# mLSTM entry: the gate columns and the broadcast products of the rows spread among the products of the token panel pair

## The reference, cut to what matters

```python
b = jnp.cumsum(lfc, axis=-1)
dmat = jnp.where(tri, b[..., :, None] - b[..., None, :] + ic[..., None, :], -jnp.inf)
m_t = jnp.maximum(jnp.max(dmat, axis=-1), m_inter)
s = jnp.einsum('bhtk,bhsk->bhts', qc, kc) * jnp.exp(dmat - m_t[..., None])
num = jnp.einsum('bhts,bhsv->bhtv', s, vc) + ...
den = jnp.sum(s, axis=-1) + ...
h = num / jnp.maximum(jnp.abs(den), jnp.exp(-m_t))[..., None]
```

## Time and profile before

| | us |
|---|---|
| runs | 2332.77, 2332.36, 2329.47 |
| median | 2332.36 |
| the profiled execution, its own time | 2332.38 |
| span of the profiled execution | 2330.7 |
| TensorE busy | 2268.5 (97%) |
| VectorE busy | 1605.5 (69%) |
| ScalarE busy | 1102.0 (47%) |

### The profile page before, as it was taken

How to read it: one execution, slowest core, us unless ns; L and a number is a source line. 1 busy time by engine, 2 the same in 40 slices (tenths; PEclk the granted TensorE clock), 3 DMA queues, 4 the chain that set the end, 5 groups by cost and what they waited for, 6 DMA issues and landing times.

```text
span 2330.7 us, 37481 instructions
## 1 busy us (share of the span) xinstructions
PE 2268.5 (97%) x13900; PEld 1973.0 (85%) x13900; DVE 1605.5 (69%) x2706; ACT 1102.0 (47%) x1748; POOL 112.1 (5%) x155
## 2 busy tenths in 40 slices
PE   9999999999999989999999999999999999999998
PEld 8998779998998779997777778888888888888888
DVE  6677857667667957777455554444546999988896
ACT  5443444445343354435555543334434666565664
POOL 0000000000000001112121201001000000000000
PEclk9999999999999999999999998999999999999999
DMA  8655126655564226664343521221221222222222
GB/s 328 228 199 181 64 100 245 232 205 200 208 230 166 82 100 217 228 222 82 73 71 74 72 99 64 73 73 64 73 82 64 91 90 81 81 81 90 81 99 91
DMA packets 83068, 301.88 MB, mean 130 GB/s; under 512 B 10404, under 2 KB 10788, under 8 KB 82468
## 3 DMA queue, kind: packets, MB, share of 16 engines
q1 hardware_dynamic: 78336, 284.72, 35.0%
q0 software_dynamic: 2048, 4.20, 3.2%
q10 hardware_dynamic: 2600, 11.81, 1.4%
HBM read 299.64 MB, written 1.05 MB: 129 GB/s over the span
## 4 chain that ended last, share of the span: by engine, by line
PE 78%; DVE 15%; ACT 4%; issue 3%; DVEq 0%; DMA 0%; ACTq 0%; another core or an unknown queue 0%
PE ps L749 49%; PE ps L797 12%; PE ps L861 4%; DVE wsplit L2158 3%; DVE work L2875 2%; PE ps L1365 2%; DVE work L2887 2%; PE ps L1226 1%; PE ps L1089 1%; PE ps L1103 1%; PE ps L764 1%; PE ps L1079 1%; DVE work L2907 1%; DVE work L2919 1%; ACT wsplit L1493 1%
## 5 line engine op out<-in xcount | busy, mean ns | idle before, releaser
L749 PE MATMUL ps<-hsplit,wsplit 128*128 128x256 f32 (+1 forms) x8376 | 1380.3, 322 | 26.8 <-DVE wsplit L2158 11.5
L749 PEld LDWEIGHTS ps<-hsplit,wsplit 128*128 128x128 f32 x8376 | 1205.6, 191 | 159.3 <-DVE wsplit L2158 18.4
L2158 DVE TENSOR_TENSOR wsplit<-ring,wsplit 128x1024 fp32r<-128x1024 f32 x465 | 576.3, 1241 | 344.4 <-ACT wsplit L1493 342.4
L1493 ACT ACTIVATE wsplit<-ring 128x1024 fp32r<-128x1024 f32 x463 | 488.6, 1058 | 514.5 <-PE ps L749 394.6
L797 PE MATMUL ps<-wsplit,fsplit 128*128 128x512 f32 x1056 | 256.5, 392 | 1.9 <-DVE fsplit L2292 1.7
L797 PEld LDWEIGHTS ps<-wsplit,fsplit 128*128 128x128 f32 x1056 | 192.6, 188 | 40.1 <-issue 3.3
L2254 DVE SCALAR_TENSOR_TENSOR work<-ring,work 128x1024 f32<-128x1024 f32 x96 | 120.3, 1253 | 1.1 <-DMA ring<-panels 1.1
L1573 ACT ACTIVATE work<-ps 128x256 f32<-128x256 f32 x88 | 33.8, 384 | 161.0 <-PE ps L749 161.0
L2378 DVE SCALAR_TENSOR_TENSOR work<-work,vec 128x256 f32<-128x256 f32 x240 | 100.9, 481 | 1.7
L749 PEld LDWEIGHTS ps<-wsplit,hsplit 128*128 128x128 f32 x768 | 96.0, 198 | 5.3 <-issue 3.8
L861 PE MATMUL ps<-work,ring 128*128 128x256 f32 x416 | 99.2, 387 | 0.0
(11 more groups left out here) (369 smaller groups left out, 2307.6 us busy)
## 6 DMA issues: line engine op xcount, KB each, us to landing
ring<-panels SPq DMA_DIRECT2D x539, 512.0 KB, 4.1
work<-latent_weights ACTq DMA_DIRECT2D x2, 2304.0 KB, 11.9
work<-rpb POOLq DMA_DIRECT2D x64, 64.0 KB, 6.6
work<-conditions ACTq DMA_DIRECT2D x6, 512.0 KB, 7.0
cst<-constants ACTq DMA_DIRECT2D x1, 1408.0 KB
work<-x SPq DMA_DIRECT2D x2, 512.0 KB, 4.8
work<-post_rows ACTq DMA_DIRECT2D x2, 512.0 KB, 4.0
cT<-ctx ACTq DMA_DIRECT2D x1, 1024.0 KB, 7.3
```

The lines of the kernel that those rows point to most:

```text
L749: ins = mm(out_, w(a), x(b), start=start and n == 0, stop=stop and n == 2, **kw)
L1493: af(wsplit[:, split_slot(name, n), 0, :], ring[:, slot, :], ACT.Copy).then_inc(high_ready, 1)
L2158: tt(parts[:, 1, :], ring[:, slot, :], parts[:, 0, :].bitcast(fp32), ALU.subtract)\
```

## The change

`token_pair` takes a function that it calls after each of its 32 steps. In `b_scores` the two broadcast products of each head no longer stand ahead of the token pair, but after its steps 1 and 4. In head 0 the 16 gate columns go from ahead of `b_scores` to after the pair's steps 0 to 15, one each, and write bank 2 in place of bank 7. The wait for `g_act_stage` moves from ahead of the pair to ahead of panel n0 + 1, which writes bank 2. The number of products and their shapes stay.

```diff
-            def token_pair(n, bank):
+            def token_pair(n, bank, between=None):
...
                         last = mm3(ps[:, bank + t // 2, (t % 2) * T:(t % 2 + 1) * T].rearrange("p (s c) -> p s c", s=2),
                                    lambda a: hsplit2[:, a, k, t * 128:(t + 1) * 128], lambda a: pair[:, :, a, k, :],
                                    k == 0, k == KD - 1)
+                        if between is not None:
+                            between(t * KD + k)
...
             pe.wait_ge(g_rows_stage, 2)
-            for which, src in enumerate((g_G, b_M)):
-                for t in range(4):
-                    for d in range(2):
-                        o = 32 * which + (2 * t + d) * 4
-                        last = mm(ps[:, 7, o:o + 4], src[0:4, d, t * 128:(t + 1) * 128], cst[0:4, K_ID:K_ID + 4],
-                                  start=True, stop=True)
-            last.then_inc(g_products_done, 1)
+
+            def gate_columns(j):
+
+                which, t, d = j // 8, j // 2 % 4, j % 2
+                ins = mm(ps[:, 2, 4 * j:4 * j + 4], (g_G, b_M)[which][0:4, d, t * 128:(t + 1) * 128],
+                         cst[0:4, K_ID:K_ID + 4], start=True, stop=True)
+                if j == 15:
+                    ins.then_inc(g_products_done, 1)
...
-                for d in range(2):
-                    last = mm(ps[:, 4 + d, :], cst[0:4, K_ID + h:K_ID + h + 1].to_broadcast([4, 128]), b_R[0:4, d, :],
-                              start=True, stop=True)
-                last.then_inc(b_rb_done, 1)
                 if h > 0:
                     pe.wait_ge(b_y_ready, h)
-                else:
-                    pe.wait_ge(g_act_stage, 2)
-                token_pair(7 + 10 * h, 6)
+
+                def between(j):
+
+                    if j in (1, 4):
+                        d = j // 4
+                        ins = mm(ps[:, 4 + d, :], cst[0:4, K_ID + h:K_ID + h + 1].to_broadcast([4, 128]), b_R[0:4, d, :],
+                                 start=True, stop=True)
+                        if d == 1:
+                            ins.then_inc(b_rb_done, 1)
+                    if h == 0 and j < 16:
+                        gate_columns(j)
+
+                token_pair(7 + 10 * h, 6, between)
...
                 full_panel("B", n0, ps[:, 1, :])
+                if h == 0:
+                    pe.wait_ge(g_act_stage, 2)
                 full_panel("B", n0 + 1, ps[:, 2, :])
...
-            flat = lambda n: ps[:, 7, 32 * n:32 * n + 32].rearrange("p (a h) -> p a h", a=8)
+            flat = lambda n: ps[:, 2, 32 * n:32 * n + 32].rearrange("p (a h) -> p a h", a=8)
```

## The result

The changed kernel takes 2347.05 us (median of 6 runs, from 2338.75 to 2350.08); the kernel before, measured beside it, 2330.91 (6 runs, 2327.44 to 2332.77). The ratio is 1.0063, 95% interval 1.0043 to 1.0082: 0.6% slower, about 15 us. The profiled execution took 2346.3 us, with a span of 2344.6.

The account below looks back on a forecast made before the run. The prediction took TensorE, busy in 97% of the span, as the bound. Head 0 +9.1, heads 1 to 3 +2.5 steady and +3.5 for falls made +15.1 on 2332.4: 2347.5 us, range 2334 to 2353.

Parts of the forecast that it names:

- (a): Head 0, gate block gone: the pair waits for VectorE's low half and starts 2.5 us after the previous pair's end.
- (b): Small products between token products: lone column 0.47 us at 2.4 GHz, 0.82 at 1.2; lone broadcast product 1.24 us.
- (c): Head 0's clock falls soon after the first broadcast product, returning 4.4 us after the last column: 34.5 us, +9.1.
- (d): Heads 1 to 3: pair waits for VectorE, +0.85 a head, +2.5 us; two clock falls instead of one, +3.5 us.
- (e): ScalarE and VectorE work behind head 0's pair stays hidden, ending at 1435.3 against the pair's 1435.8; no cost.
- A: Rival for the spread products: the seam is free, the clock still falls; head 0 +2.4 us, total 2335; chance 0.08.
- B: Rival for the spread products: the seam costs, the clock holds; +0.5 us, total 2332.9; chance 0.07.
- C: Faster rival: no seam cost, and token products between hold the clock up; total 2326.3 us; chance 0.05.

Follow-up runs that it names:

- the run with fours: The changed kernel, still with 4-row products, but four gate columns at a time after steps 3, 7, 11 and 15; 2336.55 us, ratio 1.0024.
- The full-row run: The changed kernel with gate columns and broadcast products contracting over all 128 rows instead of 4, constant operand zero in the rest; 2324.92 us, ratio 0.9985.
- the run with the broadcast products alone: The kernel before with only the broadcast products spread, after steps 1 and 4 of each pair; gate columns in a block ahead of the rotation; 2338.3 us, ratio 1.0029.

## Why the prediction was right

2347.5 us was forecast and 2347.05 measured. By its steps:

- *(a)* Start of head 0's pair 2.5 us after the previous one: 1399.58 - 1396.86 = 2.72. Right; TensorE waits there for VectorE's low half, as said.
- *(b)* A lone column 0.47 us at 2.4 GHz and 0.82 at 1.2: measured 0.50 and 0.81. A lone broadcast product 1.24: the steady 0.90 a head of the run with fours, against 0.85 forecast, bears it out. (Two sums of this step are off by 0.01: 1.23 and 0.83 come out of their terms.) The full-row run shows that it is a seam between row counts, and nothing of fp32 beside fp32r: there the column costs 0.22, its price in the block. The run with fours shows that it is paid once for each visit. The Trainium skill ("TensorE: Matmul & The Clock Gate", Part 3, what overlaps and what doesn't) has a weight load overlap a running matmul only where the row groups differ. The traces agree with it in part at most. Between 128 and 4 rows, which share rows 0 to 3, the load did not run ahead (1402.68, as its product), but with the same 128 rows on both sides it did (load 1408.07, product 1408.19). That 4 rows count as another row group than the 128 around them was the prediction's reading, and the lone columns' price contradicts it.
- *(c)* Head 0, 34.5 us: measured 34.02 and 33.98. The time at full clock was forecast as 3.5 us and was 3.8 and 2.8 in the two profiles; the low tail after the last column was forecast as 4.4 and was 3.9 and 2.2. The step's account of the clock was too simple: it put broadcast products and columns on one footing. The runs show two roles: over 4 rows, the broadcast products go ahead of the fall, and with columns behind them the clock stays down. And it had the clock return only with token products without a break, where in the run with fours it rose in the last group of columns.
- *(d)* Steady part +0.85 a head: right (+0.90). The falls were undersized: two in three heads at 2.5 us, +3.5 us over before. In both profiles all three heads fell, in the first for 10.2, 6.8 and 3.4 us, which by 16.77 for a head without a fall cost 4.5, 3.0 and 1.5 us; in the second 1.5 each. Heads 1 to 3 together lost 10.3 us in the first profiles (59.36 against 49.09) and 4.2 in the second (54.77 against 50.57), where 6.0 was forecast. This is the mis-sized term; with two profiles of each kernel its mean over executions stays open.
- *(e)* Hidden work stayed hidden, by 0.80 us where 0.5 was forecast. The full-row run shows that this cover has an end: there the pair is 14.5 us shorter, and 1.3 us of the chain show.

The total comes as close as 0.5 us by luck. The mechanism held in the main, but the changed kernel's own runs spread from 2338.75 to 2350.08, and its second set, beside the kernel before again, had a median of 2342.84 (+0.47%, 11 us). The sum was made against a profile of before with 4.3 us of falls in the first layer and the longer low stretch at head 0; against the second profile of before, head 0 costs 33.98 - 22.34 = 11.6 us, not 9.1, and the heads 4.2. The stage as a whole lost more than the 15.1 forecast in both pairs of profiles (18.8 and 15.8 us); in the first pair the changed kernel's profile had none of the first layer's falls, which offset it.

Of the rivals, A (free seams) and B (clock holds) fall at once by the rows after; C needed a column under 0.3 us and a clock that never falls; the full-row version has both, and takes 2324.92 us where C gave 2326.3.

## What to carry to other kernels

Small TensorE products spread among large ones were not free here, though TensorE had no gap on either side of them. Look whether their row count differs from their neighbours', since each visit cost 0.28 us more at 2.4 GHz (0.50 against 0.22), and see what the granted clock does after them. A product over 4 rows can run over all 128 if its constant operand is zero in the rest; here that turned +0.6% into -0.15%, and with one reordering on ScalarE into -0.35%. The spreading itself was not what gained: over 128 rows the old order came to the same -0.15%. And when a move is timed by two profiles, first subtract the falls of the clock in stages that the change doesn't touch.

## What the runs showed of the hardware

- A matmul over 4 rows next to one over 128: its weight load starts only with it (1402.68). It took 0.50 us for a product that costs 0.22 between its like or over 128 rows, 0.81 at half clock.
- The clock fell while TensorE was busy without a gap (1403.9 in the earlier trace rows). The Trainium skill ("TensorE: Matmul & The Clock Gate", Part 1, what's actually happening) has activity release the throttle. The trace doesn't agree if activity is read as the profile's busy time, which was 2.60 us of 2.60 ahead of this fall.
- Broadcast products of 512 columns over 4 rows ran ahead of falls in every head of the changed kernel, though two heads of the run with fours, and head 0 of the run with the broadcast products alone, had them without a fall. The same products over 128 rows left the clock at 1.00 in all 12 heads of the three versions that spread columns over 128 rows, and in all 8 of the two profiles with columns over 4. The seams alone don't make the fall: in those two profiles head 0 has 16 lone columns with two seams each. For the block of columns the number of rows did not matter: the clock fell after it over 128 rows too (1403.6).
- The length of a low stretch is not a property of the kernel alone: the same block gave 13.7 us in one execution of the kernel before and 6.8 in another.
